# A weight stream in rows of 4 KB instead of 12 KB: each expert unit begun as three transfers

## What is computed

```
def swiglu(t, w1, w3, w2):
    return (jax.nn.silu(t @ w1) * (t @ w3)) @ w2

def moe_swiglu(x, router, w1, w3, w2):
    ...
    for e in range(N_EXPERTS):
        out = out + combine[:, e:e + 1] * swiglu(t, w1[e], w3[e], w2[e])
```

## Time and profile before

| | us |
|---|---|
| three runs | 1850.02, 1851.67, 1856.31 |
| median | 1851.67 |
| span of the profiled execution | 1855.0 |
| PE busy in it | 1756.9 (95%) |
| DVE busy | 730.5 (39%) |
| ACT busy | 367.3 (20%) |
| bytes moved by DMA | 473.34 MB, 255 GB/s over the span |

### The profile page before, as it was taken

One profiled execution on the slowest core, in us unless ns is written; L12 is line 12 of the kernel. 1 busy time (PEld: TensorE's weight loads), 2 busy tenths in 40 slices (PEclk: granted clock), 3 DMA queues, 4 the chain that ended last, 5 costly groups with the idle time before them and its releaser, 6 DMA issues.

```text
span 1855.0 us, 64483 instructions
## 1 busy us (share of the span) xinstructions
PE 1756.9 (95%) x29182; PEld 1551.9 (84%) x29182; DVE 730.5 (39%) x1820; ACT 367.3 (20%) x856; POOL 2.9 (0%) x12
## 2 busy tenths in 40 slices
PE   8999988999999999998898998999899999999997
PEld 6887877587776888787758998988899899999996
DVE  6975745211110597664524222232223222232224
ACT  6443412102000734242212000100000000000000
POOL 0000000000000000000000000000000000000000
PEclk9999999999999999999998999999999999999999
DMA  8323212533433423222273999999999999999994
GB/s 324 107 92 114 92 65 85 212 111 143 161 144 143 152 102 107 98 92 70 92 306 145 384 412 361 427 426 426 424 425 411 391 427 427 425 427 425 427 426 180
DMA packets 55115, 473.34 MB, mean 255 GB/s; under 512 B 5280, under 2 KB 5568, under 8 KB 20960
## 3 DMA queue, kind: packets, MB, share of 16 engines
q1 hardware_dynamic: 53456, 463.49, 62.3%
q10 hardware_dynamic: 1184, 5.75, 0.8%
q0 software_dynamic: 368, 2.64, 0.4%
HBM read 470.80 MB, written 1.06 MB: 254 GB/s over the span
## 4 chain that ended last, share of the span: by engine, by line
PE 82%; DMA 10%; issue 3%; DVE 3%; ACT 1%; SPq 0%; DVEq 0%; ACTq 0%
PE bank L1083 21%; PE bank L1006 11%; PE bank L860 11%; DMA ring<-in_moe 10%; PE bank L533 8%; PE bank L910 7%; PE bank L930 4%; PE bank L892 3%; PE bank L874 3%; PE bank L694 2%; PE bank L1033 2%; PE bank L1073 1%; PE bank L673 1%; PE bank L683 1%; PE bank L645 1%
## 5 line engine op out<-in xcount | busy, mean ns | idle before, releaser
L1083 PE MATMUL bank<-arena,ring 128*64 128x80 f32 (+2 forms) x8192 | 311.6, 233 | 21.2 <-issue 10.3
L1083 PEld LDWEIGHTS bank<-arena,ring 128*64 128x64 f32 x8192 | 296.2, 137 | 27.0 <-issue 16.3
L2048 DVE TENSOR_TENSOR arena<-arena,bank 128x80 f32<-128x80 f32 (+2 forms) x224 | 53.1, 237 | 522.3 <-ACT arena L1373 522.2
L1373 ACT ACTIVATE arena<-bank 128x80 f32<-128x80 f32 (+3 forms) x246 | 61.7, 251 | 902.6 <-PE bank L1083 714.4
L1083 PE MATMUL bank<-arena 128*64 128x80 f32 (+2 forms) x6144 | 226.5, 233 | 3.7 <-issue 2.3
L860 PE MATMUL bank<-xT,ring 128*128 128x256 f32 x1024 | 227.8, 381 | 0.0
L1083 PEld LDWEIGHTS bank<-arena 128*64 128x64 f32 x6144 | 217.9, 137 | 6.5 <-issue 4.1
L860 PEld LDWEIGHTS bank<-xT,ring 128*128 128x128 f32 x1024 | 193.0, 190 | 30.7 <-issue 5.0
L1006 PE MATMUL bank<-arena,ring 128*64 128x80 f32 (+2 forms) x4096 | 167.3, 233 | 3.7 <-issue 3.7
L1006 PEld LDWEIGHTS bank<-arena,ring 128*64 128x64 f32 x4096 | 157.6, 138 | 7.7 <-issue 4.2
L533 PE MATMUL bank<-xT,ring 128*128 128x256 f32 x704 | 156.3, 383 | 7.8 <-DMA ring<-in_w_in 7.8
(11 more groups left out here) (411 smaller groups left out, 1557.7 us busy)
## 6 DMA issues: line engine op xcount, KB each, us to landing
ring<-in_moe SPq DMA_DIRECT2D x128, 1536.0 KB, 13.2
arena<-in_moe SPq DMA_DIRECT2D x96, 1536.0 KB, 12.0
ring<-in_ffn SPq DMA_DIRECT2D x22, 1536.0 KB, 6.5
ring<-in_w_gate SPq DMA_DIRECT2D x32, 1024.0 KB, 4.9
ring<-in_w_in SPq DMA_DIRECT2D x14, 1536.0 KB, 6.7
ring<-in_w_branch SPq DMA_DIRECT2D x8, 1024.0 KB, 4.8
ring<-in_w_out SPq DMA_DIRECT2D x8, 1024.0 KB, 6.0
arena<-ml_rows ACTq DMA_DIRECT2D x4, 512.0 KB, 4.3
```

The source lines that it names most:

```text
L1083: last = mm(bank[c:c + STRIP, g * CAP:g * CAP + n], w[:, at:at + STRIP], rhs[:, kt, 0:n], start=(kt == 0), stop=(kt == KT - 1), skip_group ...
L1373: f(ff_sl[:, i % 2, 0:n], bank[:, 0:n], ACT.Silu).then_inc(S["h_silu"], 1)
L2048: tt_(ACTIVE_H[:, i, 0:PLACES[e]], ff_sl[:, s % 2, 0:PLACES[e]], bank[:, CAP:CAP + PLACES[e]], ALU.mult)\
```

## The change

A unit is no longer loaded by one transfer of 128 rows of 12 KB but by three transfers of 128 rows of 4 KB, one for each third, issued one behind the other into the same slot. All three add to the slot's semaphore, which thus rises by 48 a unit, and PE waits for the full 48. The waits of SP and the order of the units are as they were. The units of `in_ffn` and of the mixers are not touched.

```
+THIRDS = 3
...
                 def block(it, at, n):
-                    loads = pe.snap(at * 16)
+                    loads = pe.snap(at * (16 * THIRDS))
...
-                        pe.wait_ge(sem_, loads + 16 * (before + 1))
+                        pe.wait_ge(sem_, loads + 16 * (before + THIRDS))
...
+            def load_thirds(slot, src):
+
+                for n in range(THIRDS):
+                    o = slice(n * D, (n + 1) * D)
+                    sp.dma_start(ex_slot[slot][:, o], src(o)).then_inc(ex_loaded[slot][0], 16)
...
-                sp.dma_start(ex_slot[s], A["moe"][0, s]).then_inc(ex_loaded[s][0], 16)
+                load_thirds(s, lambda o: A["moe"][0, s][:, o])
...
-                sp.dma_start(ex_slot[s % EX_RING], src).then_inc(ex_loaded[s % EX_RING][0], 16)
+                load_thirds(s % EX_RING, lambda o: src[:, o])
...
-                            sp.dma_start(ex_slot[i], all_units[bass.ds(row, 1)].rearrange("o p c -> p (o c)"))\
-                                .then_inc(ex_loaded[i][0], 16)
+                            load_thirds(i, lambda o: all_units[bass.ds(row, 1), :, o].rearrange("o p c -> p (o c)"))
```

## The result

The changed kernel takes 1875.9 us (median of four runs, 1870.9 to 1880.9) where the kernel before takes 1852.4 (1850.0 to 1856.3): a ratio of 1.0115 on record, 95% interval 1.0095 to 1.0134. That is +21 us; the two medians alone are 23.5 us apart. The forecast was +10. The sign and the place were right; the size was under half of what came.

What follows compares the result with a forecast made beforehand. The DMA engines' rate was taken to bound the expert stage's end, with PE later in some experts. +11.4 us for 4 KB rows and -1 us for instruction fetches made +10: 1851.7 to 1862 us, range 1847 to 1882.

Steps and rivals of the forecast that it cites:

- The bound and the path: Expert stage: DMA's rate sets its end, last landing at about 1829.8 us; PE is later only in some experts.
- 139 units on the path: Expert stage: 44 units in 1150 to 1311 us plus 95 in 1480 to 1829.8 pay 0.082 us each, 11.4 us.
- 85 units covered by PE's longer blocks: Expert stage: units that move while PE is late, PE's 27.1 us blocks hiding the slower 26.4 us of DMA.
- the rate of 4 KB rows: Full-queue stream in the expert stage: taken as 417 GB/s, 3.772 us a unit, +0.082, making +11.4 us.
- my bounds (426 and 402): GB/s limits for the 4 KB stream: 426 means no cost, 402 means +0.22 us a unit, 31 us in all.
- the Trainium skill's overhead: About three cycles a packet: 16 more packets per engine and unit x 3.5 ns, 7.8 us in all, time 1858.
- SP: right that it costs nothing: SP's three issues for one, at 0.333 us each, 1.0 us a unit of the 3.69 it takes; cost taken as 0.
- Instruction fetches: PE's "issue" stops, 19.2 us in the expert stage: fetches wait less behind 4 KB packets, taken as -1 us.
- rival (B): Entries of experts 0, 1 and 4: shorter fetch waits make the kernel faster, 1846 us; chance 0.12 as a gain beyond 0.3%.
- Rival (A): Expert stream: full queue hides packet overhead, 4 KB rows also at 426 GB/s, 1851 us; 0.30 shared with cancelling fetch gains.
- Rival (C): Full queue: each transfer's end costs 0.1 us, 28 us on top of 11.4, 1891 us; 0.08 shared with the 402 GB/s bound.
- signs for "right": 415 to 420 GB/s in 1500-1800, blocks there 26.2 to 26.6 us, 88-column blocks still 27, 672 SP issues at 0.33 us.

## Why the prediction was half right

**The bound and the path: right, the count of units by errors that cancel.** The edit touches a stage in which DMA is the last to finish, and what it costs there comes out at the end. I counted 139 units on the path; with the unit's true price that gives 139 x 0.149 = 20.7 us, where +21.3 were measured (19.9 between the two spans).

In detail the path was another. I had called 85 units covered by PE's longer blocks. The blocks of 88 columns were still PE's, 27.08 us on the chain (1373.20 to 1400.28), but such a block covers a slower stream only as far as DMA had stood idle in it, and that was little: the earlier trace rows show 424 in 1150-1200, and the fourth expert ran at 423. From 1000 us to the last landing DMA moves this:

```profile
DMA packets 31288, 341.83 MB, mean 412 GB/s; under 512 B 3472, under 2 KB 3472, under 8 KB 3472
DMA packets 93786, 341.87 MB, mean 402 GB/s; under 512 B 10416, under 2 KB 10416, under 8 KB 93744
```

The first line is the kernel before, the second the changed one. At 426 GB/s these bytes take 802 us, of the 830 that passed; at 409.6 they take 835, of 850. So all 217 units of the stretch pay 0.149, 32 us together, and 12 of these are taken up by time in which DMA had been below its full rate (27 us before, 15 now). By parts, the same working gives for the first expert +4 paid and -6 taken up, for the second and third +7 and -3, and from the fourth on +21 and -3: not the 95 units behind 1480 us paid there but all 138, while from the second expert to 1311 only 4.2 us came out and not 44 x 0.149 = 6.6.

**The step that failed: the rate of 4 KB rows, the term from which the 11.4 us came.** I took 417 GB/s, +0.082 us a unit; it is 409.6, +0.149, within my bounds (426 and 402) and nearer to the lower. At my own 139 units that is 20.7 us in place of 11.4. The choice rested on two rows that both flatter. The 414 of the earlier trace rows has ScalarE's loads in it, 3.55 MB in 440 packets, among them rows longer than 4 KB. The 421 of the earlier trace rows are single slices of 0.75 us. The changed kernel shows what such a slice is worth, in 1550-1580, in the middle of a stream that runs at 410 throughout:

```profile
GB/s 421 415 388 426 415 404 410 415 399 410 415 410 399 415 410 404 421 415 393 415 415 404 410 421 404 404 415 404 404 415 410 404 421 415 393 415 415 404 415 415
```

A slice holds some 75 packets and reads in steps of one packet, 5.5 GB/s: 388 to 426 where the rate is 410. I took its upper readings for the rate. The one look that was longer than a slice and had 4 KB rows alone, 402 with a transfer's start in it, deserved the most weight: half way to 421 it would have given 411. This weighing is made with the result at hand.

The estimate that the Trainium skill's overhead gives (DMA: Bandwidth & Descriptors, "Why small descriptors are slow (HBM only)", three cycles a packet, 3.5 ns) fell short further: the runs show 9.3 ns, 2.6 times as much, for rows of 12 KB down to 2 KB (10 for 24 KB, from a difference of only 0.035 us a unit).

**SP: right that it costs nothing, wrong on how it looks.** Its issues in the changed kernel no longer take 0.333 us (durations min/median/max ns, in 1600-1640):

```profile
L2173 SPq DMA_DIRECT2D ring<-in_moe x20: 333/936/2732, 1602.6 to 1638.1; - x20
```

and the page's chain of waits now names it second only to PE:

```profile
PE 70%; SPq 18%; issue 5%; DVE 3%; DMA 2%; ACT 1%; DVEq 0%; ACTq 0%
```

An obvious rival is that SP itself now sets the pace. The run with one transfer of the same packets speaks against it. SP issues a third as often, the issue takes up to 1.85 us in the same stretch, and over the stage SP stands still 479 us, waiting for PE to free a slot; the kernel is as slow:

```profile
L2196 SPq DMA_DIRECT2D arena<-in_moe x6: 1254/1660/1846, 1599.2 to 1633.0; - x6
SPq L2196 <- PE bank L1006: 479.2, 194, 6.9
```

With 256 packets a unit (the run with 8 and 4 KB rows) the issues are near 0.333 us again:

```profile
L2173 SPq DMA_DIRECT2D ring<-in_moe x15: 332/333/546, 1600.0 to 1634.7; - x15
```

And the run with 2 KB rows shows that it is not the number of packets in a transfer that makes an issue long. The same 768 packets take SP 0.37 us at the stage's begin, where a unit lands 9.4 us after its issue, and 3.7 us later, where it lands after 17.0:

```profile
L2181 SPq DMA_DIRECT2D ring<-in_moe x12: 367/368/368, 1009.8 to 1076.6; - x12
L2196 SPq DMA_DIRECT2D ring<-in_moe x6: 2272/3726/5847, 1607.1 to 1639.6; - x6
```

So an issue is long because SP is held up behind a stream that already runs, and not for the work of issuing. The engines never lack for it: in 1525-1625 of the changed kernel a third lands 13.8 us after its issue, while the engines need 3.84 us for a whole unit. What the limit that holds SP counts was not found.

**Instruction fetches: wrong, no gain.** PE's stops (waits in 1000-1860, us in total, times, longest) were 19.2 us in the earlier trace rows and are 19.7:

```profile
PE bank L1084 <- DMA ring<-in_moe: 24.6, 59, 1.2
PE bank L1084 <- issue: 14.0, 11, 2.0
PE bank L1007 <- issue: 5.7, 5, 1.9
```

They were 25.1 with 2 KB rows and 16.0 with rows of 24 KB: shorter packets do not let a fetch through sooner. If anything it is the other way, but there is one trace of each, and with rows of 12 KB and a shorter lead the sum is 13.6, so what sets it stays open. My -1 us was nothing, and rival (B), for which the sum should have come under 10, is out (its 1846 also takes off 10 us where its own text has 9). The rule of the Trainium skill named beside (B) (the same page, "Queues, rings and completion order") would, by the working in (B), have taken some 9 us off these stops; no row shows that.

**Rival (A)** is out by 410 against 426. **Rival (C)**, a price for each transfer's end, is out by one transfer being as slow as three. The sign that I had given for it, a rate below 410 with a full queue, was met all the same (409.6), so it was no sign of (C) alone. Of the signs for "right" only the blocks of 88 columns held: a block of 80 columns took 26.89 us and not 26.2 to 26.6, and the rate was under 415. The fit of 2.0 us fixed plus bytes over 436 GB/s, cited beside (C), stands in the Trainium skill for transfers that GpSimd issues (the same page, "Anatomy of one DMA — SWDGE (gpsimd) path"). All transfers of `in_moe` are issued by SP.

## What to carry to other kernels

Where a stream of weights sets the pace, count the packets that each DMA engine moves. With a full queue three transfers of 4 KB rows cost no more than one, but each row is a packet with a fixed price, here 9.3 ns against 460 ns for 12 KB (2%), 6% for 4 KB and 11% for 2 KB. Rows of 12 KB are near the end of what there is to win (24 KB brought the rate from 426 to 430, and the time went up), and the lead of the slots (two units of seven were worth 10 us) is worth more than the last per cent of rate. To price a rate, divide the bytes of a stretch of several microseconds by its time; single slices of under a microsecond scatter by 5%, and it is easy to pick the wrong ones.

## What the runs showed that I had not expected

- With transfers over 48 and 32 partitions instead of 128 the engines need 0.84 us for a 12 KB packet in place of 0.46: 236 GB/s in place of 426, and the kernel a third slower. Cause not tested.
- SP's issue of a transfer gets long when the stream runs far behind it: in 1600-1640 it is 0.33 us with 256 packets a unit, 0.94 at the median for each of three with 384, 1.3 to 1.7 for one with 384, and 3.7 for one with 768, which took 0.37 at the stage's begin. The chain of waits then runs over SP although the DMA engines are the bound.
- The length of the queue did not change the rate: 426 GB/s with landings of 18.7 us and of 11.3 us.
